# Neighbourhood heads: values in column halves, feature-major outputs, exponentials over the scores in PSUM

## The reference

```python
sc = jnp.einsum('brqhd,brwchd->bhrqwc', qb, kb) + bias[None]
sc = jnp.where(valid[:, None, :], sc, -jnp.inf)
pr = jax.nn.softmax(sc.reshape(*sc.shape[:4], -1), axis=-1).reshape(sc.shape)
return jnp.einsum('bhrqwc,brwchd->brqhd', pr, vb)
...
return jnp.concatenate([ret_out, na_out], axis=-1) @ w_out
```

## Time and profile before

| | us |
|---|---|
| median of 3 runs | 1010.84 |
| lowest and highest run | 1009.25, 1011.47 |
| the profiled execution | 1008.57 |
| its span | 1006.7 |
| PE busy in the span | 966.7 |
| POOL, ACT, DVE busy | 676.6, 605.5, 471.2 |

### The profile page before, as it was taken

The page is one execution under the profiler, slowest core; times in us unless marked ns, Lnnn a source line. Parts: engine busy times, 40 slices in busy tenths (PEclk is TensorE's granted clock), DMA queues, the critical chain, the costliest instruction groups (busy, mean ns, idle before and its releaser), DMA issues. The chain is left out here.

```text
span 1006.7 us, 15876 instructions
## 1 busy us (share of the span) xinstructions
PE 966.7 (96%) x6093; PEld 847.1 (84%) x6093; DVE 471.2 (47%) x990; ACT 605.5 (60%) x1130; POOL 676.6 (67%) x538
## 2 busy tenths in 40 slices
PE   6999998999999999999999899999999999899998
PEld 5888788999999797888877799999987887688777
DVE  4735334453434645776944544444346131233552
ACT  7636656555555676877967664555557464685531
POOL 5977725766666785797778575757777855485664
PEclk9999999999999999999998999999999999999999
DMA  9684424776554556457456356565555537544221
GB/s 334 224 236 150 157 84 147 233 240 196 189 188 168 175 143 201 143 161 245 165 178 219 130 186 210 167 209 168 175 175 199 178 120 269 192 127 166 85 84 42
DMA packets 124952, 177.64 MB, mean 176 GB/s; under 512 B 13185, under 2 KB 86797, under 8 KB 124685
## 3 DMA queue, kind: packets, MB, share of 16 engines
q1 hardware_dynamic: 120701, 168.91, 51.7%
q10 hardware_dynamic: 4176, 7.71, 2.2%
HBM read 175.47 MB, written 5.24 MB: 180 GB/s over the span
## 5 line engine op out<-in xcount | busy, mean ns | idle before, releaser
L531 POOL TENSOR_TENSOR wlo<-raw,whi 128x512 fp32r<-128x512 f32 (+1 forms) x502 | 656.4, 1342 | 301.0 <-ACT whi L1217 285.1
L548 PE MATMUL PS<-Th,whi 128*128 128x256 f32 (+2 forms) x1000 | 285.8, 286 | 3.5 <-DVE Tl L1755 2.8
L549 PE MATMUL PS<-Tl,whi 128*128 128x256 f32 (+2 forms) x1000 | 282.5, 283 | 0.0
L550 PE MATMUL PS<-Th,wlo 128*128 128x256 f32 (+2 forms) x1000 | 282.4, 283 | 0.0
L1217 ACT ACTIVATE whi<-raw 128x1024 fp32r<-128x1024 f32 (+1 forms) x144 | 150.7, 1047 | 161.6 <-PE PS L550 122.5
L1830 DVE SCALAR_TENSOR_TENSOR arena<-PS,cols,arena 128x255 f32<-128x255 f32 (+1 forms) x272 | 118.5, 477 | 192.1 <-ACT arena L1350 165.6
L545 PE MATMUL PS<-whi,Th 128*128 128x512 f32 x480 | 194.2, 405 | 9.7 <-DVE Tl L1804 3.3
L548 PEld LDWEIGHTS PS<-Th,whi 128*128 128x128 f32 (+2 forms) x1000 | 191.3, 191 | 9.9 <-issue 5.9
L549 PEld LDWEIGHTS PS<-Tl,whi 128*128 128x128 f32 (+2 forms) x1000 | 191.4, 191 | 1.7 <-issue 0.7
L550 PEld LDWEIGHTS PS<-Th,wlo 128*128 128x128 f32 (+2 forms) x1000 | 191.2, 191 | 0.1
L547 PE MATMUL PS<-whi,Tl 128*128 128x512 f32 x480 | 188.9, 393 | 0.0
(11 more groups left out here) (242 smaller groups left out, 1038.7 us busy)
## 6 DMA issues: line engine op xcount, KB each, us to landing
raw<-in_ffn_w_up_dram SPq DMA_DIRECT2D x44, 1024.0 KB, 5.1
raw<-in_w_in_dram SPq DMA_DIRECT2D x23, 1024.0 KB, 5.2
raw<-in_ffn_w_down_dram SPq DMA_DIRECT2D x22, 1024.0 KB, 4.9
raw<-in_c_w_in_dram SPq DMA_DIRECT2D x16, 1024.0 KB, 5.3
raw<-in_ab_w_in_dram SPq DMA_DIRECT2D x14, 1024.0 KB, 6.6
raw<-in_c_w_out_dram SPq DMA_DIRECT2D x8, 1024.0 KB, 5.1
raw<-in_ab_w_out_dram SPq DMA_DIRECT2D x4, 1024.0 KB, 5.8
raw<-in_c_w_in_dram SPq DMA_DIRECT2D x8, 512.0 KB, 5.3
```

The costliest lines, as they stand in the source:

```text
L531: i = nc.gpsimd.tensor_tensor(lo_of(n)[:, c:e], raw[n % NRAW][:, c:e], hi_of(n)[:, c:e].bitcast(F32), ALU.subtract)
L548: mm(o, wh, ah, start=first, stop=False)
L549: mm(o, wh, al, start=False, stop=False)
L550: return mm(o, wl, ah, start=False, stop=last)
```

## The change

For the non-causal heads (the causal ones keep their path):

- ScalarE writes the exponentials to PSUM, over the scores in banks 4 and 5, and no longer to sc.
- A new VectorE function normed() takes the reciprocals of the two row sums and multiplies the exponentials from PSUM into sc. It runs for both heads of a pair before the hook "a" (so before ret_gate in pair 0). TensorE's turn() waits for it, and so do the scores of the next pair.
- The values have the two heads of a pair in two column halves of the array: stationary the 64 value columns of a head (128x64), moving the turned probabilities of 256 queries. Output features lie on partitions: DH * j in bank 7. Four matmuls of 256 columns in place of eight (of 64) per pair. Probabilities have four buffers; two lie where the retention's values were.
- The output is feature-major, so turn_na, na_write and their 8 transposes go. ScalarE's pair_hi(p) and VectorE's finish(p) make Th and Tl of a pair straight from bank 7.
- The values of pair p run between the two turns of pair p+1 as before, those of the last pair in the middle of out_last.
- turn_ret moves from k = 2 to k = 3 of its slot. On ScalarE the split of the first FFN slot moves from between the last two copies to behind them, ahead of pair_hi(3).

```diff
+        ptn = pt + [view(3072 + 512 * i, 4, P) for i in range(2)]
...
                 def turn(i):
-                    pe.wait_ge(*at("a_exp", (tag, i)))
+                    pe.wait_ge(*at("a_exp" if causal else "a_nrm", (tag, i)))
...
-                            o = tr(PS[:, 6, (2 * t + c) * P:(2 * t + c + 1) * P], sc[i % 2][:, t, c * P:(c + 1) * P], ident)
+                            j = 2 * t + c if causal else 2 * c + t
+                            o = tr(PS[:, 6, j * P:(j + 1) * P], sc[i % 2][:, t, c * P:(c + 1) * P], ident)
...
+                def pair_values(p):
+
+                    for i in (2 * p, 2 * p + 1):
+                        pe.wait_ge(*at("a_pt", (tag, i)))
+                    if p:
+                        pe.wait_ge(*at("T_lo", ("y0b", p - 1)))
+                    for c in range(NT):
+                        for j in range(2):
+                            o = mm(PS[DH * j:DH * j + DH, 7, (p % 2) * S:(p % 2 + 1) * S], heads[2 * p + j][2](c),
+                                   ptn[(2 * p + j) % 4][:, 2 * c:2 * c + 2, :].rearrange("p a b -> p (a b)"), start=c == 0, stop=c == NT - 1)
+                    o.then_inc(*done("a_v", (tag, 2 * p + 1)))
...
-                            pe.wait_ge(*at("a_sc", (tag, 2 * p - 1)))
+                            pe.wait_ge(*at("a_sc" if causal else "a_nrm", (tag, 2 * p - 1)))
...
-                    elif p:
+                    elif p and causal:
                         values(2 * p - 2)
                         values(2 * p - 1)
+                    elif 0 < p < n:
+                        pair_values(p - 1)
...
-                slot_tm(("nv", hf), 0, 4 * hf, hf == 0, hf == 1, mid=turn_ret if hf else None, mid_at=2)
+                slot_tm(("nv", hf), 0, 4 * hf, hf == 0, hf == 1, mid=turn_ret if hf else None, mid_at=3)
...
-                         (3, "b"): (lambda: turn_na(0),)}))
-            out_last("mo0", 4, (12, 14), [("y0b", 1), ("y0b", 3)], mid=lambda: turn_na(2))
+            out_last("mo0", 4, (12, 14), [("y0b", 1), ("y0b", 3)], mid=lambda: na_pair(3))
...
                         nk = P if causal and t == 0 else S
-                        e = act.activation(sc[i % 2][:, t, 0:nk], sc[i % 2][:, t, 0:nk], ACT.Exp,
+                        to = sc[i % 2][:, t, 0:nk] if causal else PS[:, 4 + i % 2, t * S:(t + 1) * S]
+                        e = act.activation(to, sc[i % 2][:, t, 0:nk], ACT.Exp,
...
+            def pair_hi(p):
+                act.wait_ge(*at("a_v", ("na", 2 * p + 1)))
+                act.activation(Th[:, 12 + p, :], PS[:, 7, (p % 2) * S:(p % 2 + 1) * S], ACT.Copy).then_inc(*done("T_hi", ("y0b", p)))
+
             pairs("na", 4, False, keyed({
...
-                (1, "m"): (U(("mo0", 0)),), (3, "m"): (U(("mo0", 1)),), (3, "b"): (lambda: T_hi("y0b", 2, 12, 4, lambda k: None),)}))
-            T_hi("y0b", 4, 12, 4, lambda k: None, 2)
+                (1, "m"): (lambda: pair_hi(0), U(("mo0", 0))), (2, "m"): (lambda: pair_hi(1),),
+                (3, "m"): (lambda: pair_hi(2),)}))
+            after_slot(("mo0", 1))
+            pair_hi(3)
...
+                def normed(i):
+
+                    s = 80 + 2 * (i % 4)
+                    dve.wait_ge(*at("a_exp", (tag, i)))
+                    lk(nc.vector.reciprocal(st[:, s + 8:s + 10], st[:, s:s + 2]))
+                    for t in range(NT):
+                        o = ts(sc[i % 2][:, t, :], PS[:, 4 + i % 2, t * S:(t + 1) * S], st[:, s + 8 + t:s + 9 + t], None, ALU.mult)
+                    o.then_inc(*done("a_nrm", (tag, i)))
+
                 def finish(p):
 
+                    if not causal:
+                        dve.wait_ge(*at("T_hi", ("y0b", p)))
+                        tt(Tl[:, 12 + p, :], PS[:, 7, (p % 2) * S:(p % 2 + 1) * S], Th[:, 12 + p, :].bitcast(F32), ALU.subtract)\
+                            .then_inc(*done("T_lo", ("y0b", p)))
+                        return
...
                         scored(2 * p + 1)
+                        if not causal:
+                            normed(2 * p)
+                            normed(2 * p + 1)
```

More of the change, by code:

```diff
@@ L860, in pairs @@
                     hook(p, "b")
+                return pair_values
             def keyed(table):
@@ L885, in mo_first @@
                 out_slot("mo0", 0, 8, ("y0a", 1))
-            def turn_na(k):
-                pe.wait_ge(*at("a_o", ("na", k + 1)))
-                to_T("y0b", hn[:, :, 512:D], k + 2, 4, k)
             pe.wait_ge(*read(("nk", 0)))
@@ L893, in _ @@
             pe.wait_ge(*at("gn_c", 1))
-            pairs("na", [operands(h, nqT, nkT, h // 2, lambda c, h=h: nv[:, c, h * DH:(h + 1) * DH]) for h in range(NH)], False,
+            na_pair = pairs("na", [operands(h, nqT, nkT, h // 2, lambda c, h=h: nv[:, c, h * DH:(h + 1) * DH]) for h in range(NH)], False,
                   keyed({(0, "a"): (lambda: na_value(0),), (0, "b"): (lambda: na_value(1),), (1, "a"): (mo_first,),
                          (2, "a"): (lambda: out_slot("mo0", 1, 10, ("y0a", 3), halves=(0,)),),
-                         (3, "a"): (lambda: out_slot("mo0", 1, 10, ("y0a", 3), halves=(1,)),),
-                         (3, "b"): (lambda: turn_na(0),)}))
-            out_last("mo0", 4, (12, 14), [("y0b", 1), ("y0b", 3)], mid=lambda: turn_na(2))
+                         (3, "a"): (lambda: out_slot("mo0", 1, 10, ("y0a", 3), halves=(1,)),)}))
+            out_last("mo0", 4, (12, 14), [("y0b", 1), ("y0b", 3)], mid=lambda: na_pair(3))
             norm_T(1)
@@ L1453, in turned @@
                     act.wait_ge(*at("a_t", (tag, i)))
-                    if i >= 2:
-                        act.wait_ge(*at("a_v", (tag, i - 2)))
+                    if i >= (2 if causal else 4):
+                        act.wait_ge(*at("a_v", (tag, i - 2 if causal else (i - 4) | 1)))
                     if causal:
@@ L1459, in turned @@
                     else:
-                        e = act.activation(pt[i % 2][:, :, :], PS[:, 6, :].rearrange("p (a b) -> p a b", a=4), ACT.Copy)
+                        e = act.activation(ptn[i % 4][:, :, :], PS[:, 6, :].rearrange("p (a b) -> p a b", a=4), ACT.Copy)
                     e.then_inc(*done("a_pt", (tag, i)))
@@ L1984, in keyed @@
                 return f
-            def na_write(p, rc, o):
-                return tt(hn[:, :, 512 + P * p:512 + P * (p + 1)].rearrange("p t (h d) -> p t h d", h=2), o, bc(rc, 3, DH), ALU.mult)
             def ret_var():
@@ L2015, in _ @@
             ret_scale()
[L2016 to L2019, removed]
+            pairs("na", 4, False, lambda i, t: nabias[:, i, 128 - 128 * t:384 - 128 * t], None,
+                  keyed({(0, "a"): (ret_gate,), (1, "x"): (lambda: T_lo("y0a", 4, 8, 2, lambda k: col("gn", k)),)}))
             post_norm(0, "ffn0", 0)
```

## The result

The changed kernel took 1004.6 us (median of 13 runs, 998.95 to 1007.94) against 1010.84 (13 runs, 1007.52 to 1013.69). The ratio is 0.9932, with a 95% interval of 0.991 to 0.9955; on 1010.84 us that is 1003.97. The forecast was 1006.4 in a range from 1004.0 to 1009.3: the direction was right, the size lay at the range's lower edge and by the ratio just outside. The ratio means 6.9 us, the forecast 4.4.

The account below looks back on a forecast made before the run. TensorE's instruction stream was taken to bound the kernel. Gains of 2.8 (values), 0.8 (output transposes) and 1.3 (end waits), less 0.5 (scaling chain), gave 4.4 us: 1010.84 to 1006.4 us, range 1004.0 to 1009.3.

Parts of the forecast that it names:

- What bounds the kernel: Whole kernel: TensorE is busy 96% of the span, so a microsecond off its stream shortens the kernel unless a wait replaces it.
- Values in column halves: Attention values on TensorE: a pair falls from 1.84 to 1.15 us, gaining 2.8 us over four pairs.
- The rule of the Trainium skill, TensorEngine Tiling (Array Packing), Restrictions: Value matmuls: column tiling switches off fast weight load; if exposed, 0.5 us more a pair, the gain 2.0 us smaller.
- No transposes of the output: TensorE in the attention: the 8 output transposes go, gaining 0.8 us.
- waits at the end: End of the attention stage: TensorE's waits for the last copy and the output's low part go, gaining 1.3 us.
- Longer chain of the probabilities: Before the probabilities' transposes: turn() waits for VectorE's scaling, 0.4 us in the third pair, 0.1 in the last; cost 0.5 us.
- The retention's gate: VectorE in pair 0: gate ends at 108.7, its moved transposes start at 109.1; covered by 0.4 us, so no cost.
- The clock: TensorE behind the attention: one fall to half speed may come or go, mean nothing, +-1.4 us in the range.
- Rival (c): Later in the kernel: one or two more clock falls give the gain back, 2 x 1.4 us, 1009.2 us; chance 0.10.
- Rival (d): End of the attention stage: its waits return in another place, 1.3 us lost, 1007.7 us; chance 0.12.
- (a): Attention values: column halves do not run side by side, 1.9 us a pair, 1.4 us gain left, 1009.4 us; chance 0.10.
- (b): VectorE's scaling from PSUM slows beside POOL to 1.3 us per 128x256 and becomes the bound, 1015.0 us; chance 0.04.

Follow-up runs that it names:

- c1: Changed kernel with the two value loops swapped and all value matmuls in one column half (output wrong): 1.88 us a pair, attention stage 52.4 us.
- a4: Changed kernel without the division by the row sums, exponentials in SBUF (output wrong): attention stage 48.13 us, 1004.21 +- 0.70 us at granted clock 0.991.
- b1: Kernel before plus only exponentials in PSUM, scaled by normed(), and the retention's transposes at k = 3: ratio 1.0024 to the kernel before.
- the 86: The 86 runs of the unedited kernel before in the later comparisons: mean 1008.75 us, mean granted clock 0.9913.
- a3: Changed kernel with exponentials left in SBUF and scaled in place there: 1005.65 +- 0.23 us at granted clock 0.991, ratio 0.9963 to the kernel before.
- a2: Changed kernel with the two value loops swapped, both matmuls of one head before the other's: 1.02 us a pair, 1004.68 +- 0.33 us at granted clock 0.991.
- b3: Changed kernel with two more dummy matmuls in each of norms 1 and 3 (4 + 1 instead of 3): mean 1002.3 us, ratio 0.9936 to the kernel before.
- b5: Kernel before with two more dummy matmuls in each of norms 1 and 3 (4 + 1 instead of 3): mean 1007.0 us, ratio 0.9985.
- b6: Changed kernel without the three dummy matmuls in each of norms 1 and 3: mean 1006.3 us, ratio 0.9975 to the kernel before.

## Why the prediction was right, and where it was not

- **What bounds the kernel.** Right. TensorE's stream lost 4.2 us and the runs 4.7 +- 0.2 at equal clock. No wait on POOL came up in the stretch; its wait for ScalarE in the stretch is 15.9 us (16.2 in the earlier trace rows).
- **Values in column halves.** 1.01 to 1.02 us a pair, where 1.15 was taken with its changes of tile; the latter show around it (0.53 and 0.59 us of transposes where 0.44 and 0.55 were). Sum per pair 0.70, forecast 0.69. The scaling from cmp_hidden's four quarters to two halves was right, and c1 shows that the reason was. The rule of the Trainium skill, TensorEngine Tiling (Array Packing), Restrictions, exposed as the prediction had it, would have cost 2.0 us; the trace shows nothing of it: with 0.5 us more a pair would take 1.5.
- **No transposes of the output; waits at the end.** From the last pair's first transposes to the norm it was 131.79 to 149.75 and is 132.62 to 146.89: 3.69 us. The forecast's terms give 0.8 + 1.3 + 2 x 0.69 = 3.5. pair_hi(3) came behind the split as worked out and held nothing.
- **Longer chain of the probabilities.** Forecast 0.5, waits in the rows 0.31 and 0.16, real price 0.8 to 0.9 (a4, b1). From the scores to the scaled head 4.38 us were forecast in the third pair and 4.05 in the fourth; the transposes came 4.43 and 4.24 us behind the scores. The first was right to 0.05 us, the second late by 0.2: what a stop costs beyond its wait was left out. Exponentials into PSUM took 0.47 to 0.48 us against 0.50; from start to start 0.49 against 0.50. The Trainium skill, ScalarE: Activation LUTs, Step-by-step, calls PSUM the lower-latency destination; here the instruction is 0.03 us shorter, and from start to start next to nothing is gained.
- **The retention's gate.** Forecast to end at 108.7 with 0.4 us of cover. VectorE's timeline after:

```profile
107.08 3.21 DVE L2044 TENSOR_TENSOR hn<-hn,arena 128x512 f32<-128x512 f32 x2
```

It ended at 110.29, its transposes started at 110.46: the cover was 0.17, since the in-place products took 1.6 us each and not 1.1 (its first rows, L2038, won back 0.8 us of that 1.0). It held, barely.
- **The clock.** This is the step that failed: "I put its mean at nothing and +-1.4 in the range". The mean was right, 0.9913 and 0.9914. The spread was sized as one fall. By its clock each run of either kernel has 1 to 9 falls of 1.3 us, and two samples of 13 runs differed by 2.2 us more than the kernels do. The forecast's level, the median of three runs (1010.84), carried that chance too: it lies 2.1 us over the mean of the 86 (1008.75). Three runs of before from 1009.25 to 1011.47 showed none of this, but the trace had 17 us at half speed in one execution, five falls in four places (157, 389, 543 and 871 us), each behind waits of TensorE, while the norm at 565 us had none; that they come and go from run to run, and that a median of a few runs carries that chance, could have been guessed there. A range of +-2 for it would have held the result. Which side the miss fell on, and that it was 0.03 us by the ratio, was luck. Rival (c) had falls as a loss that the edit brings; the mean clocks show neither a loss nor a gain.
- Rival (d), waits back in another place, didn't come; (a) is what one half alone does (c1), (b) what a source in SBUF does (a3); the edit has neither.

## What to carry to other kernels

Where matmuls have only 64 output features, give the two halves of the array one head each and let the moving side be long; the gain is in both halves being in use (0.7 to 0.9 us of a pair's 1.7 to 1.9), hardly in fewer instructions (0.1) and not in their order. Take what a VectorE multiplication reads from PSUM when GpSimd works beside it. When a kernel's runs spread by 1%, compare at equal granted clock: there half a microsecond can be told, where the ratio of 13 runs to 13 was off by 2.2 us.

## What the runs showed of the hardware

- Two heads' matmuls in different column halves overlap even when all four records of one stand ahead of all four of the other: 1.02 us for the eight in a2, 1.88 in one half in c1. How the array does that no run shows.
- A one-input multiplication from SBUF, 128x256 fp32, takes 0.31 us alone and up to 1.32 us beside POOL's subtraction; from PSUM 0.44 us either way (a3, after).
- Filling 1.7 us more of the waiting in each of two norms with dummy matmuls raised the mean clock by 0.003 (b3, b5), taking the existing ones away lowered it by 0.005 (b6).
